# The second expert matrix of a mixture-of-experts stage loaded from ScalarE's queue, one expert ahead

## The reference, cut to what matters

```python
def moe(xn, router_w, router_b, w1, b1, w2, b2):    # 256 tokens, 32 experts, top 4
    logits = xf @ router_w + router_b
    top_v, top_i = lax.top_k(logits, TOP_K)
    gates = softmax(top_v)
    ...                                             # rows gathered per expert
    h = xb @ w1[e] + b1[e]                          # w1[e]: 1024 x 2048
    gate, lin = jnp.split(h, 2, axis=-1)
    gate = jnp.minimum(gate, 7.0)
    lin = jnp.clip(lin, -7.0, 7.0)
    act = gate * jax.nn.sigmoid(1.702 * gate) * (lin + 1.0)
    y = act @ w2[e] + b2[e]                         # w2[e]: 1024 x 1024
    ...                                             # weighted by the gate, summed per token
```

## Time and profile before

| what | value |
|---|---|
| median of 3 runs | 1324.57 us (1323.24 to 1327.51) |
| the profiled execution | 1326.32 us, its span 1324.6 us |
| TensorE busy | 1236.4 us (93%) |
| DVE, ScalarE busy | 321.7 us (24%), 199.6 us (15%) |
| moved from HBM | 441.37 MB, 334 GB/s over the span |
| chain that ended last | TensorE 57%, DMA 35%, DVE 5%, ACT 2% |
| first product (L1243), `ring` units | 342.6 us busy, 28.3 us idle before, released by DMA |
| expert loads | 192 of 2 MB, median 24.8 and 24.9 us from issue to landing |

### The profile page before, as it was taken

One profiled execution on the slowest core, in us unless ns is written; L12 is line 12 of the kernel. 1 busy time (PEld: TensorE's weight loads), 2 busy tenths in 40 slices (PEclk: granted clock), 3 DMA queues, 4 the chain that ended last, 5 costly groups with the idle time before them and its releaser, 6 DMA issues.

```text
span 1324.6 us, 15983 instructions
## 1 busy us (share of the span) xinstructions
PE 1236.4 (93%) x6465; PEld 592.6 (45%) x6465; DVE 321.7 (24%) x778; ACT 199.6 (15%) x373; POOL 14.2 (1%) x52
## 2 busy tenths in 40 slices
PE   5999979999979999999999999999999999999996
PEld 4888867788753333333333333233333223333332
DVE  3553445221141112121121111111211211121213
ACT  2221342102021111111111111111111111111111
POOL 4000000000000000000000000000000000000000
PEclk9999979999979999999999999999999999999998
DMA  7443201495377999999999999999999999999993
GB/s 216 128 127 104 72 2 50 135 401 177 131 278 317 427 429 431 427 427 430 427 427 427 429 430 427 428 430 427 427 428 430 429 427 391 420 430 428 428 428 148
DMA packets 70420, 443.11 MB, mean 335 GB/s; under 512 B 10091, under 2 KB 44214, under 8 KB 45814
## 3 DMA queue, kind: packets, MB, share of 16 engines
q1 hardware_dynamic: 65666, 442.16, 81.1%
q10 hardware_dynamic: 4724, 0.55, 0.3%
HBM read 441.37 MB, written 1.31 MB: 334 GB/s over the span
## 4 chain that ended last, share of the span: by engine, by line
PE 57%; DMA 35%; DVE 5%; ACT 2%; issue 1%; ACTq 0%; DVEq 0%; SPq 0%
DMA ring<-in_moe_w 35%; PE ps L1243 20%; PE ps L840 9%; PE ps L1270 7%; PE ps L860 7%; PE ps L1183 2%; PE ps L1201 2%; PE ps L1232 1%; PE ps L867 1%; PE ps L1011 1%; PE ps L1189 1%; ACT arena L816 1%; PE ps L1142 1%; PE ps L1125 1%; PE ps L986 0%
## 5 line engine op out<-in xcount | busy, mean ns | idle before, releaser
L1243 PE MATMUL ps<-ring,arena 128*64 128x512 f32 x1536 | 342.6, 599 | 28.3 <-DMA ring<-in_moe_w 28.3
L1243 PEld LDWEIGHTS ps<-ring,arena 128*64 128x64 f32 x1536 | 106.3, 137 | 264.4 <-issue 205.2
L1729 DVE TENSOR_SCALAR arena<-ps 128x512 f32<-128x512 f32 x32 | 22.1, 692 | 458.8 <-PE ps L1243 458.8
L812 ACT ACTIVATE arena<-arena 128x512 f32<-128x512 f32 x32 | 20.1, 629 | 719.4 <-DVE arena L1729 719.4
L1270 PE MATMUL ps<-ring,arena 128*64 128x512 f32 x512 | 113.4, 596 | 0.0
L1270 PE MATMUL ps<-arena 128*64 128x512 f32 x512 | 113.4, 596 | 0.0
L1243 PE MATMUL ps<-arena 128*64 128x512 f32 x512 | 112.6, 592 | 0.0
L840 PE MATMUL ps<-arena,ring 128*128 128x256 f32 x480 | 108.1, 388 | 4.6 <-DVE arena L1329 3.0
L840 PEld LDWEIGHTS ps<-arena,ring 128*128 128x128 f32 x480 | 93.0, 195 | 19.0 <-issue 6.2
L860 PE MATMUL ps<-ring,arena 128*128 128x256 f32 x320 | 70.3, 380 | 4.1 <-DVEq L1591 3.1
L1742 DVE COPY arena<-ps 128x512 f32<-128x512 f32 x32 | 22.1, 692 | 202.7 <-PE ps L1270 202.7
(11 more groups left out here) (267 smaller groups left out, 861.2 us busy)
## 6 DMA issues: line engine op xcount, KB each, us to landing
ring<-in_moe_w SPq DMA_DIRECT2D x128, 2048.0 KB, 24.8
arena<-in_moe_w SPq DMA_DIRECT2D x64, 2048.0 KB, 24.9
ring<-in_w_in SPq DMA_DIRECT2D x13, 1024.0 KB, 5.3
ring<-in_wkv_x SPq DMA_DIRECT2D x8, 1024.0 KB, 5.5
ring<-in_w_out SPq DMA_DIRECT2D x4, 1024.0 KB, 5.0
ring<-in_wq_x SPq DMA_DIRECT2D x4, 1024.0 KB, 8.3
ring<-in_wo_x SPq DMA_DIRECT2D x4, 1024.0 KB, 5.0
arena<-in_x SPq DMA_DIRECT2D x2, 512.0 KB, 3.8
```

The lines of the kernel that those rows point to most:

```text
L812: s.activation(sg[:, :], gg[:, :], ACT.Sigmoid, scale=1.702).then_inc(sem("sig_ready"), 1)
L1243: ins = t.matmul(ps[c * BLK:(c + 1) * BLK, 4 + b, :], xeT[:, col:col + BLK], w[:, f0:f0 + 512], start=False, stop=(k == KC - 1), skip_grou ...
L1729: v.tensor_scalar(gg[:, :], ps[:, 4, :], 7.0, None, ALU.min).then_inc(sem("gate_ready"), 1)
```

## The change

The method `second_units` is no longer called for the first pass on SyncE. ScalarE gets a function `next_second(e, it, par)` which, ahead of the elementwise work of iteration `it`, waits until iteration it-1 has used unit 4, issues unit 4 of expert e+1, waits until iteration it-1 has used unit 5, and issues unit 5 of expert e+1. It runs in iterations 1 to 30, so it loads experts 2 to 31; the second matrices of experts 0 and 1 are loaded by SyncE in the early part, as before. The order by use that the last six experts had on SyncE is kept for units 0 to 3 (`head`, `tail_units`) and does not hold for units 4 and 5, which are one expert ahead throughout. ScalarE's loop is written with its first and last iteration outside and two iterations in its body; `expert(it)` is the old body. For further passes SyncE loads the first two second matrices itself.

```diff
@@ SyncE, expert loop @@
                     head(2 * r + n, it, n % 2, True)
                     after = sp.snap(2 * r + (n + 1))
                     tail_units(after, after, 1 - n % 2)
-                    second_units(after, after, 1 - n % 2)
             head(E - LAST - 1, E - LAST - 1, (E - LAST - 1) % 2)
             for e in range(E - LAST, E):
                 head(e, e, e % 2)
                 tail_units(e, e, e % 2)
-                second_units(e, e, e % 2)
...
                 with sp.Fori(1, np_) as q:
+                    for par in range(2):
+                        second_units(par, sp.snap(q * E + par), par)
                     with sp.Fori(0, E // 2) as r:
                         for par in range(2):
                             e, it = sp.snap(2 * r + par), sp.snap(q * E + 2 * r + par)
                             head(e, it, par)
                             tail_units(e, it, par)
-                            second_units(e, it, par)
@@ ScalarE, expert loop @@
+            w2v = a["moe_w2"]
+
+            def next_second(e, it, par):
+
+                for half in range(2):
+                    dst, landed_ = unit(1 - par, 4 + half)
+                    if half == 0:
+                        act.wait_ge(eused, it * 4)
+                    else:
+                        act.wait_ge(sem("yy_filled"), it)
+                    act.dma_start(dst, w2v[e + 1, half]).then_inc(landed_, 16)
+
+            def expert(it):
+
+                act.wait_ge(sem("gate_ready"), it + 1)
+                s.activation(sg[:, :], gg[:, :], ACT.Sigmoid, scale=1.702).then_inc(sem("sig_ready"), 1)
...
             with act.Fori(0, np_) as q:
-                with act.Fori(0, E) as e:
-                    it = act.snap(q * E + e)
-                    act.wait_ge(sem("gate_ready"), it + 1)
...
+                expert(act.snap(q * E))
+                with act.Fori(0, (E - 2) // 2) as r:
+                    for n in (1, 2):
+                        it = act.snap(q * E + 2 * r + n)
+                        next_second(act.snap(2 * r + n), it, n % 2)
+                        expert(it)
+                expert(act.snap(q * E + (E - 1)))
```

More of the change, by code:

```diff
@@ L807, in _ @@
             np_ = act.value_load(npass[0:1, 0:1], min_val=1, max_val=PASSES)
-            with act.Fori(0, np_) as q:
-                with act.Fori(0, E) as e:
-                    it = act.snap(q * E + e)
-                    act.wait_ge(sem("gate_ready"), it + 1)
[L812 to L818, removed]
+            w2v = a["moe_w2"]
[10 more added lines that the diff above has]
+                s.activation(sg[:, :], gg[:, :], ACT.Sigmoid, scale=1.702).then_inc(sem("sig_ready"), 1)
+                act.wait_ge(sem("GT_filled"), it + 1)
+                s.activation(GT[:, :], ps[:, 7, 0:T], ACT.Copy).then_inc(sem("GT_ready"), 1)
+                act.wait_ge(sem("xe_filled"), it + 2)
+                s.activation(xe[:, :], ps[:, 6, :], ACT.Copy).then_inc(sem("xe_ready"), 1)
+                act.wait_ge(sem("acT_filled"), it + 1)
+                s.activation(acT[:, :], ps[:, 7, :], ACT.Copy).then_inc(sem("acT_ready"), 1)
+            with act.Fori(0, np_) as q:
+                expert(act.snap(q * E))
[5 more added lines that the diff above has]
+                expert(act.snap(q * E + (E - 1)))
             for i in range(NT):
```

## The result

The changed kernel takes **1335.45 us** (median of 4 runs, 1332.94 to 1338.95) against 1325.18 for the kernel before (4 runs, 1323.24 to 1327.51). The ratio is 1.0083 with a 95% interval of 1.0065 to 1.0102: slower by 10 us. The forecast was 1335.0.

What follows compares the result with a forecast made beforehand. Bytes were taken to pace the middle and TensorE the last experts, balanced to 10 us at the end. Issue terms 0; the filled dip (-2.2) enters the end's sum, +10.4 on the median 1324.57: 1335.0 us, range 1321 to 1347.

Steps and rivals of the forecast that it cites:

- What bounds the kernel: Expert stage: the middle goes at the pace of the bytes, 29.4 us per expert; in the last experts TensorE is the bound.
- SyncE, ScalarE: 0: Issue queues: SyncE loses 60 issues and ScalarE gains 60, its table load still covered; no time gained or lost.
- The dip filled, -2.2 us for the end of the bytes: At 1121 to 1124 ScalarE's queue fills a DMA gap; weights end at 1298.5 instead of 1300.7.
- Sharing by halves: Last six experts: SyncE's and ScalarE's queues each get half the DMA rate while both hold work.
- The sum at the end: Last experts: late unit 3 of expert 30 plus 43.5 us of TensorE work ends at 1321.1 against 1310.67, +10.4 us.
- order alone: End of the stage: with one-queue service only the new last unit, unit 3 of expert 31, counts; +5.3 us.
- the wait that I had named: Near the end: TensorE waits for unit 3 of expert 30, landing at 1277.6, with 43.5 us of work behind it.
- (A): Rival, last experts: both queues served like one, in order of issue; +5.3 us, 1329.9 us; 12%.
- (B): Rival, whole kernel: only 20 us of SyncE's issue time moves, which nobody waits for; 1324.6 us; 10%.
- (C): Rival, expert stage: two queues cost DMA rate; 2% is +12 us on top of 10.4, 1347 us; 15%.
- (D): Rival, last experts: first-matrix units overtake, so expert 31's second matrix lands last; -7.3 us, 1317.3 us; 10%.

Runs made afterwards that it cites:

- e1: Changed kernel, but SyncE again issues the second matrices of the last six experts, in order of use; 1325.70 us, ratio 1.0007.
- e2: Kernel before, all loads on SyncE, but second matrices issued one expert ahead to the very end; 1329.24 us, ratio 1.0039.
- e3: Changed kernel, but in the last six experts ScalarE issues the next expert's second matrix only after unit 1 is used; 1332.47 us, ratio 1.0067.
- e5: As e3, but in the last six experts ScalarE issues a second matrix only when unit 2 of the same expert has landed; 1328.44 us, ratio 1.0031.

## Why the prediction was right, point by point

**What bounds the kernel.** Right. In all kernels the middle moved 425 to 428 GB/s (one window, 404.5 to 1121), whatever its queues, and e1 shows that moving the middle's loads leaves the time within 2.6 us.

**SyncE, ScalarE: 0.** Right in the sum. One step was beside the point: of the 32 table loads in the loop only the first is left. ScalarE has 342 instructions instead of 373, and is busy 159.9 us instead of 199.6, 40 less. What in the new form of the loop does it was not tested; in e1 the last seven experts run in a loop of one expert per turn, as before, and have no table load either, so it isn't the two experts per turn; ScalarE idles before the sigmoid for longer instead (22.8 us and more where 21.5 were), and nobody waited for those loads before either.

**The dip filled, -2.2 us for the end of the bytes.** Right in kind, and too small. Counted from the start of expert 1, the weights ended after 1294.8 - 424.8 = 870.0 us instead of 1300.7 - 426.9 = 873.8: -3.8. The dip was wider than the 3 us that I took: in the kernel before, the windows of 3 us from 1118, 1124 and 1127 show 360, 360 and 399 GB/s, which at 427 is 1.1 us more, 3.3 in all. The 0.5 us left are within what slices of 427 to 431 GB/s make of 870 us.

**Sharing by halves.** Right, to about 1 us. ScalarE's six issues between 1190 and 1270 us in the changed kernel (line 817), and below them all issues of line 415 in e2 from 1200 to 1300, one queue:

```profile
DMA to landing us min/median/max: 13.5/16.9/20.4
```

```profile
DMA to landing us min/median/max: 20.2/23.5/33.7
```

By halves the first of a pair should land after 2 x 4.9 + 2.7 = 12.5 us, and the second, issued 3.5 us later, after 12.5 + 9.8 - 3.5 = 18.8. Read one by one, the pair of expert 30 took 13.8 and 20.2 us and that of expert 31 took 13.5 and 19.8, each 1.0 to 1.4 us over halves. In e2, on one queue, no unit of those 100 us took less than 20.2. That they were not served in order of issue, two transfers of the changed kernel show. SyncE issued units 2 and 3 of expert 29 at 1210.8 and 1211.3 (unit 1 of 29 is in the same window), and ScalarE unit 4 of expert 30 at 1227.9:

```profile
L415 SPq DMA_DIRECT2D arena<-in_moe_w x2: 430/431/432, 1210.8 to 1211.3; - x2
...
DMA to landing us min/median/max: 18.0/24.3/33.6
```

```profile
L817 ACTq DMA_DIRECT2D ring<-in_moe_w x1: 339/339/339, 1227.9 to 1227.9; - x1
...
DMA to landing us min/median/max: 13.8/13.8/13.8
```

Unit 3 of 29, the one of 33.6 us, landed at 1244.9; unit 4 of 30, issued 16.6 us behind it, at 1241.7, 3.2 us ahead of it. The rule of the Trainium skill (page "DMA: Bandwidth & Descriptors", section "Queues, rings and completion order", engines going round their queues by packets) agrees with these numbers; here both queues had packets of 16 KB.

**The sum at the end.** The size was right (+10.4 forecast; +10.3, then +9.2 by the medians, 9.2 and 11.1 by the stages), and its halves too: +5.3 for order alone, where e2 measured +5.2, and about +5 for sharing, where the change less e2 gives 3 to 6. But in the first profile it was not the wait that I had named, and there the agreement of the sum is in part luck. Unit 3 of 30 wasn't waited for: it landed at 1271.85, 2.3 us before TensorE came to it. Unit 3 of 29 was waited for, 2.34 us and then 16 matmuls that took 1.7 us too long, and from there TensorE was the bound. 1244.98 + 43.5 + 27.4 + 1.7 = 1317.6, and the product ended at 1317.77. The term that the sum lacked is the clock: at half rate after a wait of more than 2 us TensorE was itself as slow as the bytes (27.43 + 1.7 = 29.1 against 29.4 us) for one expert. By the wait that I had named the stage would have grown by 1271.85 + 43.5 - 424.79 - 883.8 = 6.8 us: my landing of unit 3 of 30, 1277.6 - 426.9 = 850.7 us after the start of expert 1, was 3.6 us late (1271.85 - 424.79 = 847.1). The wait for 29 and the slow clock made it 9.2. In the second profile the named wait was the last one; its unit landed after 849.5 us, 1.2 early, and 1.7 us of slow clock behind it made up for that.

**The rivals.** (A), in order of issue, is refuted by the landing times (not by e3), though its price is right for one queue (e2). (B), only issue time moves: out, and with it, as a forecast of the sum, the rule of the Trainium skill that I set beside it (same page, section "Issuing engines are not separate DMA queues", more issuing engines save issue time alone). The bytes do go through the same 16 engines, as that section has it, and at the same rate here, but the order in which they land changed, and that was worth 10 us. (C), the rate: the slices of the stage show 427 to 431 GB/s up to the one in which the weights end, as before. (D), faster: out; the last bytes were unit 3, with 22.9 us from their end (1294.8) to the end of the product.

## What to carry to other kernels

Where transfers keep the engines busy to the end, ask what lands last and how much work stands behind it: the same bytes at the same rate, in another order, cost 5 us here, and eight or ten experts in order of use instead of six gained 2 to 3. The second queue was here not a lane of its own but about half of the same one: what was put there was served beside the first queue's work, and took from it though it was needed later. If it must be used, issue its transfers when those that are needed sooner have landed or nearly so. e5 did it when unit 2 of the same expert had landed, and got back 4 to 5 of e3's 8.9 us; against one queue in order of use it still lost 4.1.

## What the runs showed of the hardware that I had not expected

TensorE's clock fell to its lower level after waits as short as 2 to 3 us in a stage in which it is otherwise busy: 16 matmuls took 5.35 instead of 3.65 us after waits of 2.04, 2.34 and 2.95 us in the changed kernel, and after waits of 2.32 and 2.94 us in its repeat. But not each time. In the changed kernel the groups after 1.96 us (at 771.48) and 2.94 us (at 1124.47) ran at full speed, and in its repeat so did four groups after 2.94 or 2.95 us (at 623.91, 770.78, 917.61 and 1064.45). What decides it the runs do not show. The kernel before, with waits of up to 1.25 us in the stage, has no such group. Where TensorE is the bound, a wait of 2 to 3 us can thus cost more than its own length: mostly 1.5 to 1.7 us more, and once 2.9 (48 matmuls at 625.26 in the changed kernel took 13.46 instead of 10.52 us). In the middle, where the bytes set the pace, the loss ate into the next waits and was worth nothing that e1 could show.
